# Two products where there were three: wide gate and up products in networks two to six

## What is computed

```python
D_FF = -(-8 * D_MODEL // (3 * 256)) * 256          # 2816

def swiglu(h, w_gate, w_up, w_down):
    return (jax.nn.silu(h @ w_gate) * (h @ w_up)) @ w_down
```

## Time and profile before

| what | value |
|---|---|
| median of 3 runs | 1774.99 us (1774.98 to 1775.22) |
| profiled execution | 1772.21 us |
| its span | 1770.6 us |
| TensorE busy | 1694.1 us (96%) |
| VectorE busy | 1178.2 us (67%) |
| ScalarE busy | 898.1 us (51%) |
| mean granted clock of TensorE | 0.988 |

### The profile page before, as it was taken

The page is one execution under the profiler, slowest core; times in us unless marked ns, Lnnn a source line. Parts: engine busy times, 40 slices in busy tenths (PEclk is TensorE's granted clock), DMA queues, the critical chain, the costliest instruction groups (busy, mean ns, idle before and its releaser), DMA issues.

```text
span 1770.6 us, 30030 instructions
## 1 busy us (share of the span) xinstructions
PE 1694.1 (96%) x11890; PEld 1578.5 (89%) x11890; DVE 1178.2 (67%) x1486; ACT 898.1 (51%) x1238; POOL 109.8 (6%) x161
## 2 busy tenths in 40 slices
PE   6988999999999999999999999989999999999996
PEld 4987999998889998999898899978999899899986
DVE  7988789867675457555676755556655675765546
ACT  4566544356543445444577544446434468643444
POOL 3110211100010000000021000000000003000000
PEclk9999999999999999999999999999999999999998
DMA  9893799937455554555442455534555442455541
GB/s 381 327 333 129 284 366 361 382 147 289 155 198 194 190 190 156 189 190 189 156 167 75 178 188 190 186 123 168 181 195 178 171 167 72 174 187 193 177 163 57
DMA packets 61924, 353.80 MB, mean 200 GB/s; under 512 B 6522, under 2 KB 9738, under 8 KB 27792
## 3 DMA queue, kind: packets, MB, share of 16 engines
q1 hardware_dynamic: 40064, 281.24, 43.9%
q0 software_dynamic: 18384, 66.66, 10.3%
q10 hardware_dynamic: 3392, 4.72, 0.9%
HBM read 349.45 MB, written 3.15 MB: 199 GB/s over the span
## 4 chain that ended last, share of the span: by engine, by line
PE 82%; DVE 8%; DMA 3%; ACT 3%; issue 2%; POOL 1%; DVEq 0%; SPq 0%; POOLq 0%; ACTq 0%
PE bank L501 25%; PE bank L502 24%; PE bank L503 24%; DVE w_lo L1562 2%; DMA shared<-in_mods 2%; PE bank L533 2%; PE bank L535 2%; PE bank L534 2%; PE bank L683 1%; ACT w_hi L1035 1%; DMA raw<-in_stream 1%; DVE shared L1584 1%; DVE shared L2139 1%; DVE x L2148 1%; POOL work L488 1%
## 5 line engine op out<-in xcount | busy, mean ns | idle before, releaser
L501 PE MATMUL bank<-a_hi,w_hi 128*128 128x256 f32 x2648 | 754.4, 285 | 18.3 <-DVE a_lo L1722 5.8
L502 PE MATMUL bank<-a_lo,w_hi 128*128 128x256 f32 x2648 | 751.0, 284 | 0.0
L503 PE MATMUL bank<-a_hi,w_lo 128*128 128x256 f32 x2648 | 750.9, 284 | 0.0
L501 PEld LDWEIGHTS bank<-a_hi,w_hi 128*128 128x128 f32 x2648 | 509.8, 193 | 24.2 <-DVE w_lo L1562 11.4
L502 PEld LDWEIGHTS bank<-a_lo,w_hi 128*128 128x128 f32 x2648 | 509.8, 193 | 2.7 <-issue 0.5
L503 PEld LDWEIGHTS bank<-a_hi,w_lo 128*128 128x128 f32 x2648 | 509.7, 193 | 0.0
L1832 DVE TENSOR_TENSOR w_lo<-raw,w_hi 128x2048 fp32r<-128x2048 f32 x144 | 330.1, 2292 | 247.3 <-ACT w_hi L1176 247.3
L1176 ACT CAST w_hi<-raw 128x2048 fp32r<-128x2048 f32 x144 | 273.9, 1903 | 270.5 <-PE bank L503 270.5
L1562 DVE TENSOR_TENSOR w_lo<-raw,w_hi 128x2048 fp32r<-128x2048 f32 x122 | 279.2, 2293 | 87.3 <-ACT w_hi L1035 87.1
L1035 ACT CAST w_hi<-raw 128x2048 fp32r<-128x2048 f32 x122 | 231.5, 1907 | 61.3 <-PE bank L503 51.4
L501 PE MATMUL bank<-w_hi,hid_hi 128*128 128x512 f32 x548 | 216.1, 394 | 4.8 <-DVE hid_lo L2319 3.0
(11 more groups left out here) (254 smaller groups left out, 1880.0 us busy)
## 6 DMA issues: line engine op xcount, KB each, us to landing
raw<-in_stream SPq DMA_DIRECT2D x266, 1024.0 KB, 4.8
shared<-in_mods POOLq DMA_DIRECT2D x104, 512.0 KB, 6.9
grow<-in_rows POOLq DMA_DIRECT2D x12, 512.0 KB, 4.0
work<-in_mods POOLq DMA_DIRECT2D x8, 512.0 KB, 9.2
bias_rows<-work ACTq DMA_DIRECT2D x1, 2048.0 KB, 21.2
x<-in_x_t SPq DMA_DIRECT2D x1, 1024.0 KB, 5.7
x<-in_x_d ACTq DMA_DIRECT2D x1, 1024.0 KB, 5.8
work<-bias_rows ACTq DMA_DIRECT2D x1, 1024.0 KB, 13.8
```

Source lines behind the costliest of these rows:

```text
L501: pe.matmul(out, w_h, v_h, start=start, stop=False, skip_group_check=True)
L502: pe.matmul(out, w_h, v_l, start=False, stop=False, skip_group_check=True)
L503: return pe.matmul(out, w_l, v_h, start=False, stop=stop, skip_group_check=True)
```

## The change

In networks two to six a gate or up slab is made by wide_slab. The high and the low activations lie side by side in one tensor a_both, [P, LCH, 2, S], so that one product with the high weights takes 512 columns, high x high into the first half of a bank and high weights x low activations into the second half. The low weights take the high activations, 256 columns, into the first half. The two halves m of the block now have a bank each, so gate and up slab each need a pair of banks (0 and 1, 2 and 3), and nothing is double any more: gate j+1 waits for gate_summed of block j, up j+1 for up_summed. VectorE adds the two halves of both banks by a tensor_reduce over the innermost of four dimensions, 1024 values in, 512 out, into gate_s or hid in SBUF. The multiplication by the row and silu then read SBUF. The first gate and up slab of network two stay as they were, in banks 2 and 3. Network one is unchanged.

```diff
-        bank = [ctx.enter_context(nc.psum_tensor(f"bank{i}", [P, 512], F32)) for i in range(8)]
+        bank_pair = [ctx.enter_context(nc.psum_tensor(f"banks{i}", [P, 1024], F32)) for i in range(4)]
+        bank = [bank_pair[i // 2][:, 512 * (i % 2):512 * (i % 2) + 512] for i in range(8)]
+        def two_sums(b):
+            return bank_pair[b][:, :].rearrange("p (m k s) -> p m s k", m=2, k=2)
...
-        a_hi = sb("a_hi", [P, LCH, S], F32R)
-        a_lo = sb("a_lo", [P, LCH, S], F32R)
+        a_both = sb("a_both", [P, LCH, 2, S], F32R)
+        a_hi, a_lo = a_both[:, :, 0, :], a_both[:, :, 1, :]
...
+            def wide_slab(slot, pair_of_banks, chunk_ready=None):
+                for c in range(CH):
+                    if chunk_ready is not None:
+                        pe.wait_ge(nl_ready, chunk_ready + c + 1)
+                    for m in range(2):
+                        w_h, w_l = weights(slot, c * 256 + m * P, P)
+                        out = bank[2 * pair_of_banks + m]
+                        pe.matmul(out[:, :], w_h, a_both[:, c].rearrange("p k s -> p (k s)"), start=(c == 0), stop=False, skip_group_check=True)
+                        mm = pe.matmul(out[:, 0:S], w_l, a_hi[:, c, :], start=False, stop=(c == CH - 1), skip_group_check=True)
+                return mm
...
                     for k, out in enumerate((bank[par], bank[2 + par])):
                         pe.wait_ge(lo_ready, ready + k)
+                        if i > 0:
+                            if j is not None or i > 1:
+                                pe.wait_ge((gate_summed, up_summed)[k], (1 if j is None else j) + (f0 - FJ - 1))
+                            elif k:
+                                pe.wait_ge(hid_done, f0 + 1)
+                            wide_slab(slot + k, k).then_inc(slab_done, 1)
+                            continue
...
                 def gate(j, par, done, first=False):
-                    if i < 2:
+                    if i == 0:
                         return
                     dve.wait_ge(slab_done, done)
...
+                    dve.tensor_reduce(pair(gate_s[:, par, :]), two_sums(0), mybir.AxisListType.X, ALU.add).then_inc(gate_summed, 1)
+                    if i == 1:
+                        return
                     if first:
                         dve.wait_ge(row_ready, rows_made(v))
-                    dve.tensor_tensor(pair(gate_s[:, par, :]), pair(bank[par][:, :]), over_pre(), ALU.mult).then_inc(gate_scaled, 1)
+                    dve.wait_ge(gate_summed, j + (f0 - FJ))
+                    dve.tensor_tensor(pair(gate_s[:, par, :]), pair(gate_s[:, par, :]), over_pre(), ALU.mult).then_inc(gate_scaled, 1)
...
-                        dve.tensor_tensor(pair(hid[:, par, :]), pair(bank[2 + par][:, :]), over_pre(), ALU.mult).then_inc(up_scaled, 1)
+                        dve.tensor_reduce(pair(hid[:, par, :]), two_sums(1), mybir.AxisListType.X, ALU.add).then_inc(up_summed, 1)
+                        dve.wait_ge(up_summed, j + (f0 - FJ))
+                        dve.tensor_tensor(pair(hid[:, par, :]), pair(hid[:, par, :]), over_pre(), ALU.mult).then_inc(up_scaled, 1)
...
-                split_to(b + 4)
-                if i == 0:
+                if i == 1:
+                    hidden(0, 0, b + 2, True)
+                    split_to(b + 4)
+                    gate_row_in(U_FFN1, 4)
+                elif i == 0:
+                    split_to(b + 4)
                     mod_half()
-                if i == 1:
-                    gate_row_in(U_FFN1, 4)
-                gate(0, 0, b + 1, True)
-                hidden(0, 0, b + 2, True)
+                    hidden(0, 0, b + 2, True)
+                else:
+                    split_to(b + 3)
+                    gate(0, 0, b + 1, True)
+                    split_to(b + 4)
+                    hidden(0, 0, b + 2, True)
```

More of the change, by code:

```diff
@@ L352, in build @@
         gate_scaled, up_scaled = sem("gate_scaled"), sem("up_scaled")
+        gate_summed, up_summed = sem("gate_summed"), sem("up_summed")
         table_ready = sem("rope_over_rms_ready")
@@ L646, in ffn @@
                     pe.wait_ge(lo_ready, b + 2)
-                    slab_pair((b, b + 1), (bank[0], bank[2]), before(APPLY_CHUNKS, ap))
+                    slab_pair((b, b + 1), (bank[0], bank[2]) if i == 0 else (bank[2], bank[3]), before(APPLY_CHUNKS, ap))
                 else:
                     pe.wait_ge(lo_ready, b + 1)
-                    feature_slab(b, bank[0], before(APPLY_CHUNKS, ap)).then_inc(slab_done, 1)
+                    wide_slab(b, 0, before(APPLY_CHUNKS, ap)).then_inc(slab_done, 1)
                     pe.wait_ge(lo_ready, b + 2)
-                    feature_slab(b + 1, bank[2]).then_inc(slab_done, 1)
+                    wide_slab(b + 1, 1).then_inc(slab_done, 1)
                 between()
@@ L1160, in silu @@
                         return
+                    if i == 1 and (j is not None or par):
+                        act.wait_ge(gate_summed, j if j is not None else par)
+                        act.activation(gate_s[:, par, :], gate_s[:, par, :], ACT.Silu).then_inc(silu_done, 1)
+                        return
                     act.wait_ge(slab_done, done)
@@ L1163, in silu @@
                         act.wait_ge(hid_done, j + (f0 - 1))
-                    act.activation(gate_s[:, par, :], bank[par][:, :], ACT.Silu).then_inc(silu_done, 1)
+                    act.activation(gate_s[:, par, :], bank[par if i == 0 else 2][:, :], ACT.Silu).then_inc(silu_done, 1)
                 def hidden_hi(j, par, done):
@@ L1815, in hidden @@
                             dve.wait_ge(hl_ready, j + (f0 - 1))
-                        dve.tensor_tensor(pair(hid[:, par, :]), pair(bank[2 + par][:, :]), over_pre(), ALU.mult).then_inc(up_scaled, 1)
+                        dve.tensor_reduce(pair(hid[:, par, :]), two_sums(1), mybir.AxisListType.X, ALU.add).then_inc(up_summed, 1)
+                        dve.wait_ge(up_summed, j + (f0 - FJ))
+                        dve.tensor_tensor(pair(hid[:, par, :]), pair(hid[:, par, :]), over_pre(), ALU.mult).then_inc(up_scaled, 1)
                         dve.wait_ge(up_scaled, j + (FJ * (i - 2) + 1))
+                        dve.wait_ge(silu_done, j + (f0 + 1))
+                        dve.tensor_tensor(hid[:, par, :], hid[:, par, :], gate_s[:, par, :], ALU.mult).then_inc(hid_done, 1)
+                        return
+                    if i == 1 and not (first and j == 0):
+                        dve.wait_ge(slab_done, up)
+                        if not first:
+                            dve.wait_ge(hl_ready, j + (f0 - 1))
+                        dve.tensor_reduce(pair(hid[:, par, :]), two_sums(1), mybir.AxisListType.X, ALU.add).then_inc(up_summed, 1)
+                        dve.wait_ge(up_summed, j)
                         dve.wait_ge(silu_done, j + (f0 + 1))
@@ L1822, in hidden @@
                     dve.wait_ge(slab_done, up)
-                    dve.tensor_tensor(hid[:, par, :], bank[2 + par][:, :], gate_s[:, par, :], ALU.mult).then_inc(hid_done, 1)
+                    dve.tensor_tensor(hid[:, par, :], bank[2 + par if i == 0 else 3][:, :], gate_s[:, par, :], ALU.mult).then_inc(hid_done, 1)
                 def hidden_lo(j, par):
```

## The result

The changed kernel takes 1786.05 us (median of six runs, 1784.47 to 1786.63); the kernel before took 1775.49 us beside it (six runs). The ratio is 1.0055, 95% interval 1.0044 to 1.0066: slower by about half a per cent, where 1767.7 us was forecast. In the two profiled executions the span grows from 1770.6 to 1783.1 us, 12.5 us longer where 7.3 shorter was expected. So 19.8 us have to be found (18.3 by the medians).

A forecast was written before the change was run, and what follows sets the result against it. TensorE alone was taken to bound the loops, with VectorE near at heads and ends. Slabs -17.1, heads +7.6, ends +1.6 and network two +0.6 made -7.3 us: median 1767.7 us, range 1762 to 1775.

The forecast's parts named there:

- the price of a pair: In gate and up slabs, a 512-column plus a 256-column product takes 346.7 ns instead of 360, saving 13.3 ns.
- 23.0 us if nothing else moved: Saving on TensorE over 108 gate and up slabs of networks two to six, 1728 pairs, before any new waits.
- the 1536 pairs that the sum counts: Pairs after the heads: 20 slabs in each of networks three to six save 17.1 us, 16 in network two 3.4.
- Rival (b): A product's cost beside its columns isn't per product; the wide one saves 2.5 ns a pair, giving 1784.3 us; chance 0.04.
- (a): The sum on VectorE runs at the scan's rate, 2.7 us, giving 1784.3 us; chance 0.08.
- The ends: At the ends of networks three to six the last down slab waits for hid_lo, 0.4 us each, 1.6 us in all.
- Rival (c): New waits let the clock fall: four falls at 2 to 3.5 us each, 1776 to 1782 us; chance 0.08.
- The sum: VectorE's addition of 1024 PSUM values into 512 after each gate or up slab takes 1.28 us.
- The heads: In networks three to six gate(1) waits for the first gate sum, behind a low half on VectorE: 7.6 us later in all.
- Network two: At its head gate(3) starts 4.0 us later; 16 slabs then save 3.4 us, so net 0.6 us slower.
- No wait for a sum inside the loops: Inside the loops the sums finish long before their banks are needed; a wait for gate_summed or up_summed there would refute the forecast.

The follow-up runs named there:

- the heads alone mended: Changed kernel with the first gate sum ahead of the low half of slab b+3 at the heads of networks three to six, ends unchanged; 1778.99 us.
- half a sum: Changed kernel with VectorE copying the first half of each bank instead of summing both, so high weights x low activations is left out; 1776.76 us.
- the kernel with both edits of order: Changed kernel with the first gate sum (heads) and hid_lo (ends) moved ahead of the low halves in VectorE's order; 1771.01 us.
- the one with everything mended: Changed kernel with VectorE's order mended at heads and ends, network two's last angles behind its loop, wide products before narrow in each slab; 1760.0 us.

## Why the prediction was wrong

**The step that failed: the price of a pair.** The prediction took 346.7 ns for 512 + 256 columns from rows in which one form follows itself, and noted that their succession doesn't occur in the trace, but kept no bound for it except 3 ns. It is 352.3 ns. The term "23.0 us if nothing else moved" was 13.3, 9.7 us less; of that, 8.6 us fall on the 1536 pairs that the sum counts. Two runs show it: three products in place of two give pairs of 360 ns and cost 8.8 us, not 23, and grouping brings 9 us back at 347.3 ns a pair. Rival (b) put a smaller gain at 0.04 and gave it another reason. That its 1784.3 us, and those of (a), lie near the measured 1786.05 is chance: the sum takes 1.22 us, not 2.7, and the pair saves 7.7 ns, not 2.5. The rule cited there, a gap of 2.5 ns per product (the Trainium skill, "TensorE: Matmul & The Clock Gate", "Back-to-back issue gap", which gives it for the isolated product), isn't what happens: in rows of their own, 256 columns still take 120 ns and 512 take 227, so 13.3 ns a product stand; it is the turn that takes the gain back.

**The ends, a mis-sized term.** 0.4 us each were forecast, 1.3 came: 3.6 us over four. The working started the up sum when TensorE had finished the bank. It had itself said that silu and the high half come 1.3 us later, against a slack of 4 us, "cost there: nothing". That holds in the loop; at the end the low half that follows them stood before VectorE's up sum until 855.21, 1.2 us after the bank was done. A delay that was declared harmless in one place was not carried to the next.

**The clock, a rival that partly came.** Rival (c) held four falls at 2 to 3.5 us. Two falls behind head waits of 2.2 us came, at 1.6 and 1.5 us; two more, near 110 and 676 us, stand at places that the change didn't lengthen by a new wait. About 5 us in all. That the first two hang on the waits is suggested by two kernels, the heads alone mended and half a sum: no half clock stands there. But the length of a wait doesn't decide. In the kernel grouped by slab the heads of networks three, four and five wait 2.21, 2.17 and 2.18 us, and these are the windows behind the three:

```profile
690.00:694.00 4.00, 3.35 (x15) 2.79 (x16) 3.83 (x6) 2.67 (x4) 0.00 (x0) 1.00 0.71 262
1000.00:1004.00 4.00, 3.85 (x10) 3.05 (x11) 3.83 (x6) 3.00 (x3) 0.00 (x0) 0.57 0.71 260
1240.00:1244.00 4.00, 3.26 (x14) 2.74 (x15) 3.83 (x6) 2.70 (x3) 0.00 (x0) 1.00 0.80 262
```

And the kernel with both edits of order has such stretches one step earlier, from 989.0 and 1535 us on, behind a row of short waits of 0.7 to 0.8 us at the change of network, as the one with everything mended has from 1522 us on. Its mean clock is 0.983, no better than the 0.984 of the changed kernel. So the stretches shift from kernel to kernel. The profile before also had a high clock, 0.988, where other executions of that kernel have down to 0.983. How much of the 5 us is the doing of this change stays open.

**Right.** The sum: 1.22 us against 1.28. The heads: gate(1) came 2.1, 2.1, 1.2 and 2.1 us later after the network's first product than before, 7.4 us in all where 7.6 were forecast. Network two: gate(3) came at 530.78, 4.5 us later than the earlier trace rows once the 1.8 us are taken off by which the whole network started late; 4.0 were forecast. No wait for a sum inside the loops.

The account of the 19.8 us: steps 8.6, longer down slabs 1.8, ends 3.6, half clock about 5, gate(3) 0.5, heads -0.2. That is 19.3; the clock is the least certain.

## What to carry to other kernels

Take a product's price from a place where its neighbours are those that it will have: here 512 and 256 columns in turn cost 5.6 ns more a pair than in rows of their own, which was 40% of the gain, and two loops in place of one bring it back. When a sum is put between a product and its user, look in the adder's queue for the long work ahead of it at every change of stage, and move the sum first: that order was worth about as much here (11 to 15 us) as the products saved (13.3 us). And a delay that the loop absorbs has to be followed to the loop's end.

## What was not expected of the hardware

- Products of 512 and 256 columns in turn run in one of two paces, 347 ns and 353 ns a pair. The first was seen in ten slabs shortly behind waits of TensorE of 0.66 to 3.18 us, though not behind every such wait, the second everywhere else and for as long as the loop ran. The slow one has a pattern over three pairs (241 + 120, 236 + 113, 232 + 118 ns). Neither the order in the pair nor the bank matters; grouped in twos or sixteens it is gone (348 to 349 and 347.3 ns a pair). The cause inside TensorE stays open.
- A reduction on VectorE that adds two PSUM values took the time of its inputs, not of its outputs: 1.22 us for 1024 values into 512, where an operation over 1024 takes 1.28 and a copy of 512 takes 0.69.
- Behind 2.2 us without work, TensorE's clock fell to half for 3.4 us in networks four and six. Behind 1.75 us before the change, behind 1.7 us with half a sum, and behind 3.18 us before gate(3) of network two in the changed kernel it didn't. What decides isn't shown.
